# One engine instead of two for the weight splits of the expert stage of a two-layer backbone

## The chip, the cores and the metric

The kernel runs on one core of a Trainium2 chip. The metric is the device time of one execution in microseconds (us). The engines named below are TensorE (PE, matmuls), VectorE (DVE), ScalarE (ACT), GpSimd (POOL) and SyncE (SP), which only issues transfers here. SBUF is the on-chip memory that they share, PSUM the eight banks that TensorE writes.

## The reference

Two layers over 256 latent and 256 context tokens of width 1024, all in float32. Layer 0 is a gated mixer and a dense SwiGLU of width 2816. Layer 1 is an attention mixer and then a top-2-of-8 mixture of SwiGLU experts over the 256 latent tokens, each expert with three 1024 x 2816 matrices:

```python
def swiglu(h, w_gate, w_up, w_down):
    return (jax.nn.silu(h @ w_gate) * (h @ w_up)) @ w_down

def moe_swiglu(h, router, w_gate, w_up, w_down):
    ...
    for e in range(N_EXPERTS):
        y = y + gates[:, e:e + 1] * swiglu(hf, w_gate[e], w_up[e], w_down[e])
    return y.reshape(b, l, d)
```

## The kernel before

**Weights come in slabs.** Every weight matrix is cut into slabs of 128 partitions x 2048 float32 (1 MB); there are 401 of them in one order, number n. SyncE loads slab n into one of six `raw` buffers. ScalarE copies it, rounded to the matmul's format, into one of three `hi` buffers (L420, `split_hi`). Then `lo = raw - hi` is written into one of three `lo` buffers (L428, `split_lo`): VectorE does the first five eighths (128x1280), GpSimd the rest (128x768), each counting on its own semaphore, `lo_dve` and `lo_pool`. TensorE waits for both counts (`slab`, L431) and makes three matmuls of each product (`product`: hi x hi, L479, then the two cross terms, L480 and L481), so that a slab is 12 matmuls of 512 columns, or 24 of 256. The last matmul of a slab raises `slab_used`.

**What a step waits for.** ScalarE's copy of slab n waits until the slab has landed and until slab n-3 is used. Both subtractions wait for that copy. The load of slab n waits until both parts of the subtraction of slab n-6 are counted (of slab n-3 in the overflow stage, where only three `raw` buffers are in turn).

**The expert stage.** The experts go in four rounds of a loop, two per round (w = 0 and 1), 33 slabs each: six blocks c of gate and up columns (slabs 0 to 21; gate and up of block c are slabs 4c to 4c+3, the last block is slabs 20 and 21), then 11 slabs of the down matrix. Each expert has 128 token slots; the overflow stage ("over") repeats one expert for the tokens that found no slot, here once. After up block c TensorE transposes the activations of block c-1 (L1843). Between slab 21 and slab 22 it transposes block 4, gathers the tokens of the next expert with small matmuls (L1815), and transposes block 5. After slab 3 of w = 1 it scatters the result of w = 0 back to the tokens (L1866, L1867), and at the end of a round that of w = 1.

**What VectorE does beside the subtraction.** Its queue is in order. Per expert: six products with silu (`act_e`, L1394), six lo parts of the transposed activations (`act_lo`, L1404), two masks of the next gather (`place`, L1381), two lo parts of the gathered tokens (L1386), two of the output (L1411), four weighted additions (L1419). The place of each in the queue is written out:

```python
for s in range(33):
    splits(st, (w, s), it=it)
    ...
    if s in (6, 10, 14, 18, 22):
        act_e(st, w, (s - 6) // 4, it)
    if s in (10, 14, 18, 22):
        act_lo(st, w, (s - 10) // 4, it)
    if s == 12 and st == "moe":
        place(0, 1 - w, it * 2 + (w + 1))
    if s == 23:
        act_e(st, w, 5, it)
        act_lo(st, w, 4, it)
```

GpSimd does nothing in the expert and overflow stages but its part of the subtraction. The gather's second half needs the PSUM bank that `act_lo` of block 4 empties.

Of the kernel before, what the change touches and what calls it, by code (L numbers as in the profile page):

```python
# [50 lines left out]
NE = 8  # L51
# [3 lines left out]
OVER = 2 * SEQ // (SLOTS + 1)  # L55
# [8 lines left out]
RAW, SPL = 6, 3  # L64
# [154 lines left out]
def build(nc, a, out):  # L219
# [3 lines left out]
    slabs, n, landed = {}, 0, [0] * RAW  # L223
# [9 lines left out]
    banks, at, signals = {}, [0] * 8, [0] * 8  # L233
    for stage, times, uses in bank_order():
# [8 lines left out]
        at = [at[b] + times * per[b] for b in range(8)]  # L243
        signals = [signals[b] + times * per_signal[b] for b in range(8)]

    with ExitStack() as ctx:
        def sem(name):
            return ctx.enter_context(nc.semaphore(name))

        def sb(name, shape, dt=F32, into=None):  # L250
            return (into or ctx).enter_context(nc.sbuf_tensor(name, shape, dt))
# [97 lines left out]
        over = sb("over", [P, 3, NE], into=zone4)  # L349
        over_i = sb("over_i", [P, 2, NE], I32, zone4)  # L350
# [19 lines left out]
        lo_pool = [sem(f"lo_pool{i}") for i in range(SPL)]  # L370
# [19 lines left out]
        h2_hi, routed = sem("h2_hi"), sem("routed")  # L390
# [6 lines left out]
        def view(t, shape):  # L397
            k, f = shape
            return t[:, 0:k * f].rearrange("p (k f) -> p k f", k=k)

        def load(sp, stage, key, src, it=0):

            n0, per, slot, _, _, depth = slabs[stage, key]
            if n0 >= depth:
                before = (n0 - depth) // SPL + 1 + it * (per // SPL)
                sp.wait_ge(lo_dve[n0 % SPL], before)
                sp.wait_ge(lo_pool[n0 % SPL], before)
                if not isinstance(it, int):

                    sp.wait_ge(hi_ready, n0 - depth + 1)  # L410
            _, k, f = src.shape
            sp.dma_start(view(raw[slot], (k, f)), src).then_inc(raw_in[slot], 16)  # L412
# [9 lines left out]
        def split_lo(eng, stage, key, size=SLAB, it=0):  # L422

            n0, per, slot, _, _, _ = slabs[stage, key]
            at = size * 5 // 8
            cols, ready = (slice(at, size), lo_pool) if eng is nc.gpsimd else (slice(0, at), lo_dve)
            eng.wait_ge(hi_ready, n0 + 1 + it * per)
            eng.tensor_tensor(lo[n0 % SPL][:, cols], raw[slot][:, cols], hi[n0 % SPL][:, cols].bitcast(F32),  # L428
                              ALU.subtract).then_inc(ready[n0 % SPL], 1)

        def slab(pe, stage, key, shape, it=0):  # L431

            n0, per = slabs[stage, key][:2]
            there = n0 // SPL + 1 + it * (per // SPL)
            pe.wait_ge(lo_dve[n0 % SPL], there)
            pe.wait_ge(lo_pool[n0 % SPL], there)
            return view(hi[n0 % SPL], shape), view(lo[n0 % SPL], shape)

        def bank(pe, stage, key, it=0):
# [10 lines left out]
        def full(eng, stage, key, it=0):  # L450

            b, _, _, r, per, closing = banks[stage, key]
            if closing is None:
                eng.wait_ge(bank_full[b], r + 1 + it * per)
            elif stage == "ffn":
                eng.wait_ge(slab_used, ffn_slab(closing, it) + 1)
            else:
                n0, per = slabs[stage, closing][:2]
                eng.wait_ge(slab_used, n0 + 1 + it * per)
            return ps[b]  # L460
# [47 lines left out]
        def ada_stage(layer, cb):  # L508

            return "late" if layer == 1 and cb in LATE else f"ada{layer}"  # L510

        def mod_rows(st, cb):

            if st == "late":
                return late_row[0:5, :]
            return (zp if st == "ada0" and cb in (2, 3) else mrow)[0:5, cb % 2, :]

        def spread(cb, who=0):

            return ("bc", cb, who) if cb in GATE_BLOCKS else ("col", cb)  # L520

        def before(layer, cb):

            if layer == 0:
                last = {4: 0, 5: 1}.get(cb, cb - 2)
                return ("ada0", spread(last, 1)) if cb >= 4 else None
            return ("ada1", spread(cb - 2)) if cb >= 2 else ("ada0", spread(10 + cb, 1))
# [41 lines left out]
        def _(sp):  # L569
            def ada(layer, key):  # L570
                cb, h = key
                load(sp, ada_stage(layer, cb), key, columns(a["ada_w"][layer], slice(4 * h, 4 * h + 4), 512 * cb, 512 * cb + 512))
# [11 lines left out]
            for stage, key in FIRST_SLABS + MIX_SLABS:  # L584
                if stage == "ab_in":
                    load(sp, stage, key, columns(a["ab_w_in"][0], slice(0, 8), 256 * key, 256 * key + 256))
                elif stage == "ab_out":
                    h, q = key
                    load(sp, stage, key, columns(a["ab_w_out"][0], slice(4 * q, 4 * q + 4), 512 * h, 512 * h + 512))
                else:  # L590
                    ada(int(stage == "ada1"), key)
# [52 lines left out]
        @block.gpsimd  # L644
        def _(pool):
            def bias(layer, cb):

                if cb == LATE[0] and layer == 1:
                    full(pool, "ukv", (3, 1))
                elif ada_stage(layer, cb) == "late":  # L650
                    full(pool, "late", spread(cb - 1))
                elif before(layer, cb):
                    full(pool, *before(layer, cb))
                pool.dma_start(mod_rows(ada_stage(layer, cb), cb)[4:5], a["ada_b"][layer:layer + 1, 512 * cb:512 * cb + 512]
                               ).then_inc(bias_in[cb % 2], 16)

            for stage, key in FIRST_SLABS + MIX_SLABS:
                split_lo(nc.gpsimd, stage, key)
                if stage in ("ada0", "ada1") and key[1] == 1 and (stage, key) not in FIRST_SLABS:
                    bias(int(stage == "ada1"), key[0])  # L660
            for key in ("g0", "u0", "g1"):
                split_lo(nc.gpsimd, "ffn_in", key)
            with pool.Fori(0, 4) as it:
                for key in ("uA", "dA", "gA", "uB", "dB", "gB"):
                    split_lo(nc.gpsimd, "ffn_loop", key, it=it)
            for key in ("u9", "d8", "g10", "u10", "d9", "d10"):
                split_lo(nc.gpsimd, "ffn_out", key)
            for j in range(6):
                split_lo(nc.gpsimd, "cd_in", j, 8 * min(256, CDIN - 256 * j))
            for h in range(2):  # L670
                split_lo(nc.gpsimd, "uq", h, 3 * 384)
            split_lo(nc.gpsimd, "ukv", 0)
            for cb in LATE:
                for h in range(2):
                    split_lo(nc.gpsimd, "late", (cb, h))
                bias(1, cb)
            for h in range(2):
                for q in range(2):
                    split_lo(nc.gpsimd, "cd_out", (h, q))

            with pool.Fori(0, NE // 2) as it:
                for w in range(2):
                    for s in range(33):
                        split_lo(nc.gpsimd, "moe", (w, s), it=it)
            pool.wait_ge(routed, 1)
            with pool.Fori(0, OVER) as j:
                more = pool.value_load(over_i[0:1, 0, bass.ds(j, 1)], min_val=0, max_val=NE)
                with pool.If(more > 0):
                    for s in range(33):
                        split_lo(nc.gpsimd, "over", (0, s), it=j)  # L690


        @block.scalar
# [790 lines left out]
        def _(pe):  # L1484
# [24 lines left out]
            def rows_of(layer, cb, h):  # L1509

                st = ada_stage(layer, cb)
                b = bank(pe, st, ("m", cb)) if h == 0 else ps[banks[st, ("m", cb)][0]]
                wh, wl = slab(pe, st, (cb, h), (4, 512))
                for k in range(4):
                    T.matmul(b[0:4, :], C4[:, 4 * h + k, :], wh[:, k, :], start=(h == 0 and k == 0), stop=False)  # L1515
                    ins = T.matmul(b[0:4, :], C4[:, 4 * h + k, :], wl[:, k, :], start=False, stop=(h == 1 and k == 3))  # L1516
                used(ins)
# [404 lines left out]
```

## Time and profile before

| | |
|---|---|
| device time, median of 3 runs | 2097.69 us (2094.6 to 2099.28) |
| span of the profiled execution | 2090.8 us |
| what lies around the span, to the median | 6.9 us |
| TensorE matmul busy | 1869.7 us, 89% |
| VectorE busy | 1321.0 us, 63% |
| GpSimd busy | 1122.4 us, 54% |
| ScalarE busy | 990.8 us, 47% |
| expert stage | 991.3 to 1931.5 us of the span |
| overflow stage | until about 2070 us |

The profile is one execution; its own time is the span and what lies around it, which the profile does not show, so 6.9 us is the difference to the median of the other runs. A row of the trace's timeline gives the start, the duration, the engine, the line, the operation with the tiles that it writes and reads, and in brackets how long the engine had been idle and what ended that. A busy TensorE is not one at its peak, since matmuls overlap: the distance from one start to the next is what counts.

### The profile page before, as it was taken

How to read it: one execution, taken by the hardware profiler on the slowest of the kernel's cores; microseconds unless marked ns; L12 is line 12 of the kernel's file. 1: busy time of each engine (PE TensorE's matmuls, PEld its weight loads, DVE VectorE, ACT ScalarE, POOL GpSimd, SP SyncE). 2: the span in 40 equal slices, each digit the busy share in tenths (PEclk: the TensorE clock that was granted, in tenths of full speed). 3: DMA queues.
4: the chain of work that ended last, by engine and by line, in shares of the span. 5: the costliest groups of instructions: out<-in, count | busy, mean ns of one | idle time of the engine just before them, and what ended most of it. 6: DMA issues, size and time to landing. Idle time of an engine off the chain costs nothing.

```text
span 2090.8 us, 24509 instructions
## 1 busy us (share of the span) xinstructions
PE 1869.7 (89%) x8695; PEld 1435.9 (69%) x8696; DVE 1321.0 (63%) x1247; ACT 990.8 (47%) x867; POOL 1122.4 (54%) x426
## 2 busy tenths in 40 slices
PE   5888969999998778996999989999999989999785
PEld 2675648888887774665677767776777767777664
DVE  5546464243345667752877869686877869686454
ACT  5443342212211434433656556565656656564453
POOL 5345331122220212330969678786969678785684
PEclk9999989999999789996999999999999999999798
DMA  9445332232322223430879789797879889795583
GB/s 354 166 137 201 121 102 82 99 110 70 120 63 71 92 73 121 162 108 30 300 269 330 279 282 342 270 325 260 301 266 330 278 279 343 269 329 200 185 297 141
DMA packets 215161, 426.41 MB, mean 204 GB/s; under 512 B 8806, under 2 KB 64648, under 8 KB 215052
## 3 DMA queue, kind: packets, MB, share of 16 engines
q1 hardware_dynamic: 210178, 420.33, 59.1%
q10 hardware_dynamic: 4234, 4.57, 0.7%
q8 instruction: 70, 1.15, 0.2%
q14 instruction: 39, 0.32, 0.0%
q0 software_dynamic: 640, 0.04, 0.0%
HBM read 423.86 MB, written 1.05 MB: 203 GB/s over the span
## 4 chain that ended last, share of the span: by engine, by line
POOL 35%; PE 33%; issue 22%; DVE 6%; ACT 3%; DMA 1%; SPq 0%; POOLq 0%; DVEq 0%; ACTq 0%
POOL lo L428 35%; PE bank L479 9%; PE bank L480 9%; PE bank L481 9%; DVE lo L428 2%; ACT hi L420 2%; PE bank L1743 1%; PE bank L1758 1%; PE bank L1515 1%; PE bank L1516 1%; DMA raw<-in_ada_w_dram 1%; PE bank L1764 1%; PE bank L1506 1%; PE bank L1501 1%; SPq L412 0%
## 5 line engine op out<-in xcount | busy, mean ns | idle before, releaser
L428 POOL TENSOR_TENSOR lo<-raw,hi 128x768 fp32r<-128x768 f32 x401 | 1112.1, 2792 | 887.2 <-ACT hi L420 887.0
L428 DVE TENSOR_TENSOR lo<-raw,hi 128x1280 fp32r<-128x1280 f32 x401 | 864.9, 2174 | 371.1 <-ACT hi L420 370.4
L420 ACT ACTIVATE hi<-raw 128x2048 fp32r<-128x2048 f32 x401 | 763.2, 1910 | 568.4 <-PE bank L481 509.9
L479 PE MATMUL bank<-hi,xgh 128*128 128x512 f32 (+1 forms) x864 | 343.7, 398 | 34.0 <-POOL lo L428 21.9
L480 PE MATMUL bank<-lo,xgh 128*128 128x512 f32 (+1 forms) x864 | 329.1, 381 | 0.0
L481 PE MATMUL bank<-hi,xgl 128*128 128x512 f32 (+1 forms) x864 | 328.6, 380 | 0.0
L479 PEld LDWEIGHTS bank<-hi,xgh 128*128 128x128 f32 x864 | 165.4, 191 | 109.3 <-issue 58.2
L481 PEld LDWEIGHTS bank<-hi,xgl 128*128 128x128 f32 x864 | 165.5, 191 | 34.0
L480 PEld LDWEIGHTS bank<-lo,xgh 128*128 128x128 f32 x864 | 165.8, 192 | 26.4
L479 PE MATMUL bank<-hi,aTh 128*128 128x512 f32 x396 | 166.9, 421 | 4.7 <-POOL lo L428 3.1
L480 PE MATMUL bank<-lo,aTh 128*128 128x512 f32 x396 | 160.1, 404 | 0.0
L481 PE MATMUL bank<-hi,aTl 128*128 128x512 f32 x396 | 159.5, 403 | 0.0
L479 PE MATMUL bank<-Hhi,hi 128*128 128x512 f32 x352 | 139.4, 396 | 2.9 <-DVE Hlo L974 2.9
L480 PE MATMUL bank<-Hlo,hi 128*128 128x512 f32 x352 | 139.6, 397 | 0.0
L481 PE MATMUL bank<-Hhi,lo 128*128 128x512 f32 x352 | 138.9, 395 | 0.0
L1138 DVE TENSOR_TENSOR am<-bank,mrow 128x512 f32<-128x512 f32 x22 | 15.2, 692 | 189.3 <-PE bank L481 189.3
L479 PEld LDWEIGHTS bank<-hi,aTh 128*128 128x128 f32 x396 | 77.2, 195 | 47.5 <-issue 32.7
L1515 PE MATMUL bank<-hi,C 128*4 128x512 f32 x192 | 82.2, 428 | 23.7 <-POOL lo L428 13.5
L479 PE MATMUL bank<-hi,Hhi 128*128 128x256 f32 (+1 forms) x256 | 82.5, 322 | 8.3 <-issue 4.6
L481 PEld LDWEIGHTS bank<-hi,aTl 128*128 128x128 f32 x396 | 77.1, 195 | 18.6
L480 PEld LDWEIGHTS bank<-lo,aTh 128*128 128x128 f32 x396 | 77.5, 196 | 14.7
L480 PE MATMUL bank<-lo,Hhi 128*128 128x256 f32 (+1 forms) x256 | 81.5, 318 | 0.0
(308 smaller groups left out, 2484.4 us busy)
## 6 DMA issues: line engine op xcount, KB each, us to landing
raw<-in_moe_w_gate_dram SPq DMA_DIRECT2D x99, 1024.0 KB, 5.2
raw<-in_moe_w_up_dram SPq DMA_DIRECT2D x99, 1024.0 KB, 5.2
raw<-in_moe_w_down_dram SPq DMA_DIRECT2D x99, 1024.0 KB, 5.0
raw<-in_ada_w_dram SPq DMA_DIRECT2D x48, 1024.0 KB, 5.2
raw<-in_ffn_w_gate_dram SPq DMA_DIRECT2D x11, 1024.0 KB, 5.4
raw<-in_ffn_w_up_dram SPq DMA_DIRECT2D x11, 1024.0 KB, 5.4
raw<-in_ffn_w_down_dram SPq DMA_DIRECT2D x11, 1024.0 KB, 4.9
raw<-in_ab_w_in_dram SPq DMA_DIRECT2D x6, 1024.0 KB, 5.3
```

The source lines that it names most:

```text
L420: nc.scalar.activation(hi[n0 % SPL][:, 0:size], raw[slot][:, 0:size], ACT.Copy).then_inc(hi_ready, 1)
L428: eng.tensor_tensor(lo[n0 % SPL][:, cols], raw[slot][:, cols], hi[n0 % SPL][:, cols].bitcast(F32), ALU.subtract).then_inc(ready[n0 % SPL], 1)
L479: nc.tensor.matmul(dst, lh, rh, start=first, stop=False, skip_group_check=True)
L480: nc.tensor.matmul(dst, lh, rl, start=False, stop=False, skip_group_check=True)
L481: return nc.tensor.matmul(dst, ll, rh, start=False, stop=last, skip_group_check=True)
L1501: filled(T.matmul(bank(pe, st, ("bc", cb, who))[:], sel[:, who, :], row, start=True, stop=True), st, ("bc", cb, who))
L1506: ins = T.matmul(b[:, 2 * j:2 * j + 2], row[:, j * P:(j + 1) * P], sel[:, :, 0], start=True, stop=True)
L1515: T.matmul(b[0:4, :], C4[:, 4 * h + k, :], wh[:, k, :], start=(h == 0 and k == 0), stop=False)
L1516: ins = T.matmul(b[0:4, :], C4[:, 4 * h + k, :], wl[:, k, :], start=False, stop=(h == 1 and k == 3))
L1743: filled(T.matmul(bank(pe, "att", ("s", i))[:], q_, k_, start=True, stop=True), "att", ("s", i))
L1758: ins = T.matmul(b[:, 0:64], pT[:, i % 2, t * P:(t + 1) * P], val, start=(t == 0), stop=(t == 3))
L1764: ins = T.transpose(b[:, t * P:(t + 1) * P], pexp[:, (i - 1) % 2, t * P:(t + 1) * P], ident[:])
```

## The change

VectorE subtracts the whole slab (128x2048) in the stages "moe" and "over"; GpSimd's loops over these stages are gone. TensorE no longer waits for `lo_pool` there. A load in these stages waits for a constant count of `lo_pool`, that of all the slabs that are still divided; for the first three loads of the experts this is a later slab than before (the last three of the attention's output matrix in place of those three slabs earlier). All other stages keep the division.

```diff
+        ALONE = ("moe", "over")
+
+        def shared_rounds(b):
+
+            return (slabs["moe", (0, 0)][0] - 1 - b) // SPL + 1
+
         def load(sp, stage, key, src, it=0):
...
                 sp.wait_ge(lo_dve[n0 % SPL], before)
-                sp.wait_ge(lo_pool[n0 % SPL], before)
+                sp.wait_ge(lo_pool[n0 % SPL], shared_rounds(n0 % SPL) if stage in ALONE else before)
...
         def split_lo(eng, stage, key, size=SLAB, it=0):
...
-            at = size * 5 // 8
+            at = size if stage in ALONE else size * 5 // 8
...
             pe.wait_ge(lo_dve[n0 % SPL], there)
-            pe.wait_ge(lo_pool[n0 % SPL], there)
+            if stage not in ALONE:
+                pe.wait_ge(lo_pool[n0 % SPL], there)
...
-            with pool.Fori(0, NE // 2) as it:
-                for w in range(2):
-                    for s in range(33):
-                        split_lo(nc.gpsimd, "moe", (w, s), it=it)
-            pool.wait_ge(routed, 1)
-            with pool.Fori(0, OVER) as j:
-                more = pool.value_load(over_i[0:1, 0, bass.ds(j, 1)], min_val=0, max_val=NE)
-                with pool.If(more > 0):
-                    for s in range(33):
-                        split_lo(nc.gpsimd, "over", (0, s), it=j)
```

## Rows read from the trace of the kernel before

**Rows 1.** The page: the span, and the chain that ended last, by line.

```profile
span 2090.8 us, 24509 instructions
...
POOL lo L428 35%; PE bank L479 9%; PE bank L480 9%; PE bank L481 9%; DVE lo L428 2%; ACT hi L420 2%; PE bank L1743 1%; PE bank L1758 1%; PE bank L1515 1%; PE bank L1516 1%; DMA raw<-in_ada_w_dram 1%; PE bank L1764 1%; PE bank L1506 1%; PE bank L1501 1%; SPq L412 0%
```

**Rows 2.** Windows: the last round of the expert loop, and the overflow stage.

```profile
core 0: us, PE busy (x) PEld busy (x) DVE busy (x) ACT busy (x) POOL busy (x), PEclk, DMA share, GB/s
...
1696.20:1931.50 235.30, 222.00 (x969) 170.14 (x968) 183.55 (x110) 143.74 (x101) 185.30 (x66) 0.95 0.83 285
1931.50:2070.00 138.50, 114.10 (x484) 87.32 (x483) 68.32 (x56) 71.15 (x50) 102.47 (x33) 0.91 0.68 228
```

**Rows 3.** Groups of instructions in the round from 1696.2 to 1931.5 us.

```profile
L428 POOL TENSOR_TENSOR lo<-raw,hi 128x768 fp32r<-128x768 f32 x66 | 185.3, 2830 | 50.3 <-ACT hi L420 50.3
L428 DVE TENSOR_TENSOR lo<-raw,hi 128x1280 fp32r<-128x1280 f32 x66 | 153.2, 2340 | 40.6 <-ACT hi L420 40.5
```

**Rows 4.** Timeline of VectorE in expert 5 (w = 1 of the third round).

```profile
1601.33 1.49 DVE L428 TENSOR_TENSOR lo<-raw,hi 128x1280 fp32r<-128x1280 f32 x1 [1.44 <-ACT hi L420]
...
1609.72 2.29 DVE L428 TENSOR_TENSOR lo<-raw,hi 128x1280 fp32r<-128x1280 f32 x1 [0.78 <-ACT hi L420]
...
1618.08 3.68 DVE L1381 TENSOR_SCALAR Pm<-slot_row,posn 128x128 fp32r<-128x128 f32 x2
...
1654.02 0.68 DVE L1404 TENSOR_TENSOR aTl<-bank,aTh 128x512 fp32r<-128x512 f32 x1
```

**Rows 5.** Timeline of GpSimd in experts 4 and 5.

```profile
1553.22 44.72 POOL L428 TENSOR_TENSOR lo<-raw,hi 128x768 fp32r<-128x768 f32 x15 [11.71 <-ACT hi L420]
...
1650.60 1.82 POOL L428 TENSOR_TENSOR lo<-raw,hi 128x768 fp32r<-128x768 f32 x1 [1.29 <-ACT hi L420]
```

**Rows 6.** Instructions of line 1473, VectorE: min/median/max ns.

```profile
L1473 DVE TENSOR_TENSOR X<-X x2: 1219/1222/1226, 2079.9 to 2081.0; 128x1024 f32<-128x1024 f32 x2
```

**Rows 7.** Timeline of ScalarE, experts 4 and 5: copies that wait for a used slab.

```profile
1551.22 1.92 ACT L420 ACTIVATE hi<-raw 128x2048 fp32r<-128x2048 f32 x1 [4.08 <-PE bank L481]
...
1593.26 1.91 ACT L420 ACTIVATE hi<-raw 128x2048 fp32r<-128x2048 f32 x1 [1.14 <-PE bank L481]
...
1664.47 1.92 ACT L420 ACTIVATE hi<-raw 128x2048 fp32r<-128x2048 f32 x1 [3.48 <-PE bank L481]
```

**Rows 8.** Timeline of TensorE in expert 5.

```profile
1596.39 0.39 PE L479 MATMUL bank<-hi,xgh 128*128 128x512 f32 x1
...
1607.58 0.60 PE L1843 MATMUL bank<-ident,ame 128*128 128x128 f32 x4
1607.93 0.48 PE L479 MATMUL bank<-hi,xgh 128*128 128x512 f32 x1
...
1644.46 0.60 PE L1843 MATMUL bank<-ident,ame 128*128 128x128 f32 x4
...
1651.39 0.65 PE L1843 MATMUL bank<-ident,ame 128*128 128x128 f32 x4 [0.69 <-DVE ame L1394]
...
1654.75 1.11 PE L1815 MATMUL bank<-Pm,h2h 128*128 128x128 f32 x8 [1.73 <-DVE aTl L1404]
...
1693.85 0.40 PE L481 MATMUL bank<-hi,aTl 128*128 128x512 f32 x1
```

**Rows 9.** Timeline of SyncE's transfers, overflow stage; 1951.14 and 1984.02 are nine loads apart.

```profile
1951.14 0.37 SPq L412 DMA_DIRECT2D raw<-in_moe_w_up_dram  x1
...
1984.02 3.46 SPq L412 DMA_DIRECT2D raw<-in_moe_w_gate_dram  x2
```

**Rows 10.** Timeline of GpSimd: its first expert slabs.

```profile
993.31 9.22 POOL L428 TENSOR_TENSOR lo<-raw,hi 128x768 fp32r<-128x768 f32 x3 [55.32 <-ACT hi L420]
```

**Rows 11.** Windows: a burst of loads, the end of slabs 20 and 21, the gather.

```profile
1216.00:1220.00 4.00, 3.98 (x18) 2.94 (x17) 2.29 (x1) 0.33 (x1) 4.00 (x2) 1.00 1.05 388
...
1648.00:1652.00 4.00, 3.31 (x29) 3.01 (x27) 4.00 (x4) 2.53 (x3) 2.71 (x2) 1.00 0.99 358
...
1656.00:1660.00 4.00, 3.66 (x18) 3.26 (x18) 3.02 (x3) 0.88 (x2) 0.38 (x1) 0.50 0.81 266
```

## The prediction

> **What bounds the kernel now.** I read the chain that ended last first: GpSimd's part of the subtraction has 35% of the span, more than any other line [rows 1]. GpSimd is only 54% busy, so this is a limit of one stage, and the windows say which: a round of two experts takes 235.3 us, with GpSimd busy for 185.3 of them; four rounds and the overflow stage (138.5 us) are half the span [rows 2].
>
> In that stage the durations are to be read, not the shares. VectorE's 128x1280 subtraction takes 1.49 us when it starts first and 2.29 us a few slabs later, 2.34 us in the mean of 66 [rows 3, 4]. GpSimd's 128x768 takes 1.82 us alone, but 15 of them in a row with no idle time take 44.72 us, 2.98 us each [rows 5]. Each engine is slow just when the other works: one waits until the other's instruction ends. So the two parts of a slab are done one after the other, in about 3.0 us, and the division buys no overlap. The two mask instructions, on only 128 elements each, show the same: 3.68 us for both [rows 4].
>
> TensorE alone is faster than that. Where its slabs are prepared ahead, four of them take 11.19 us (1596.39 to 1607.58), 2.80 each, and the transposes behind them 0.35 us, 11.54 in all; the next three such blocks took 36.88 us (1607.58 to 1644.46), 12.29 each [rows 8]. In the down part ScalarE's copies, each of which waits for a used slab, tell the same: 14 slabs from 1551.22 to 1593.26 us, 3.00 us each [rows 7]. So TensorE is held back by 0.2 us per slab, by the pair VectorE and GpSimd.
>
> **What the change does to a slab.** GpSimd's 1.82 us of work and all mutual waiting go; VectorE gets 768 more elements. No 128x2048 subtraction is in the trace. From below: 128x1024, alone, takes 1.22 us and 128x1280 takes 1.49 us [rows 4, 6], 1.05 ns per element, so 2048 elements take 2.29 us. From above: the stage's mean of 2.34 us scaled by 1.6 is 3.74 us [rows 3]. I take 2.29 us, because the mean holds waiting for GpSimd, which then has no work.
>
> Latency first: TensorE reaches slab n 5.60 us after it has used slab n-3. The copy takes 1.92 us [rows 7], the subtraction 2.29, the handovers about 0.1: 4.3 us, 1.3 us to spare. Where a product and a transposed lo part stand between two subtractions (two instructions of at most 0.68 us, started 0.60 us apart), the next is 0.7 us late, still inside. Throughput: four slabs cost VectorE 4 x 2.29 + 1.2 = 10.4 us against TensorE's 11.54. So TensorE becomes the bound, at 2.80 us per slab.
>
> **What it is worth, per round of two experts.**
> - Three blocks of each expert: 36.88 - 3 x 11.54 = 2.26 us [rows 8], twice: 4.5 us.
> - From slab 22 of w = 0 to slab 3 of w = 1: 42.04 - 14 x 2.80 = 2.8 us [rows 7].
> - Slabs 1 to 7 of w = 0, held back in the same way by 0.2 us: 1.4 us.
> - Slabs 23 to 32 of w = 1: from the copy at 1664.47 to the last matmul, which starts at 1693.85 and occupies TensorE for 0.23 us more, 29.6 us; less 28.0 gives 1.6 us [rows 7, 8].
> - Between slabs 21 and 22 TensorE waits 0.69 us for VectorE's product and then 1.73 us for the lo part that ends at 1654.70 [rows 4, 8]. VectorE comes to these with two subtractions before it, each after GpSimd's. With its queue no longer late the first wait goes. The lo part moves only by 0.8 us: the subtraction of slab 23 in front of it waits for its copy. 0.8 us, twice: 1.6 us.
> - At the start of a round the other way: VectorE comes to slab 0 late, from its additions, when GpSimd has done its part, and its 2.29 us are 0.5 us more than what it does now. A loss of 0.5 us.
>
> Sum 11.4 us, four rounds: 46 us. The wait of TensorE at the scatter of w = 1 stays: it hangs on additions that follow the subtraction of slab 5, whose end was VectorE's own 2.29 us after its copy, as it will be.
>
> **The overflow stage.** With three buffers a load waits for the subtraction three slabs back, so load, copy and subtraction form a ring. Nine loads took 32.88 us, 10.96 us per turn of three [rows 9]. GpSimd ends 3.1 us after the copy (a third of 9.2 [rows 10]), VectorE alone will after 2.29: 0.8 us per turn, 11 turns: 9 us. At then 10.1 us per turn TensorE's 8.4 us and the transfers have room.
>
> **What moves.** The first three expert loads wait for later slabs, the last of which GpSimd finishes at 993.31 - 55.32 = 937.99 us; they are needed at about 991 us [rows 10]. At 2.7 us per load [rows 11] six take 16 us, 37 us before that: nothing. The cover would be gone if they were more than 50 us late. GpSimd issues no transfers in these stages, so nothing is queued behind its removed instructions; TensorE loses a wait, and nobody gains one.
>
> **Transfers.** At 2.80 us a slab needs 375 GB/s. In a burst, with all engines at work, they moved 388 GB/s, 2.70 us per slab; in another window, with the transfer engines 0.99 busy, only 358 GB/s, 2.93 us per slab [rows 11]. I take the first, since in the second the loads were asked for no faster, and TensorE's pauses let them refill six buffers. The Trainium skill ("SBUF — State Buffer", summary of rules) would have 358 GB/s assumed between HBM and SBUF: by it the transfers would bound, as in the rival below. The first window is above that figure.
>
> Sum: 46 + 9 = 55 us, plus 1 us in the first round and the first overflow slab, which wait for GpSimd's end and not for VectorE's: 56 us. The profiled execution goes from 2090.8 to 2035 us; with the 6.9 us around it, 2041.7 us against the median of 2097.69.
>
> **Rivals.**
> - *VectorE stays late in the gate and up part* (its extra instructions and waits for ScalarE sit between subtractions with little to spare), the down part gains. Against it: 1.1 us spare in each block. Lost: 4 x (4.5 + 1.4) = 24 us, so 2066 us.
> - *The transfers bound.* If they sustain only the 358 GB/s of that window and the lead of six buffers doesn't cover it, 264 slabs lose 0.13 us: 34 us, so 2076 us. Against it: at 0.13 us per slab, 15 slabs use up 2 us of lead, and the lead is over 10 us (a load is issued when slab n-6 is subtracted).
> - *VectorE becomes the bound, slower.* Were the subtraction really 3.74 us, the 66 of a round would take 247 us; with about 30 us of other work VectorE would need 277 us of a round of 235.3: 4 x 42 + 11 x 0.6, so 2272 us. It decides from about 2.8 us per subtraction, where four and the 1.2 us beside them fill the 12.29 us of a block. For it speaks only the mean row; against it the 1.49 us when undisturbed.
> - *No change*: 3.0 us per slab is also near what a transfer takes, and if that set the pace nothing would move. Against it: the copies wait for TensorE (the releaser in brackets), not for data [rows 7].
> - *TensorE's clock.* Between slabs 21 and 22 the granted clock falls to 0.50 (1.2 GHz instead of 2.4) after TensorE's waits [rows 11]; over a round it is 0.95 [rows 2], some 12 us lost. Shorter waits may keep it up. If a third of it goes: 16 us more, so 2026 us. It can also fall for longer. The Trainium skill ("TensorE: Matmul & The Clock Gate", what's actually happening) says that idleness lowers the clock and activity restores it; by that rule shorter waits can only help, and the same 2026 us or less would come out.
>
> **The numbers.** Forecast 0.77, late in the gate part 0.09, transfers 0.03, clock 0.06, VectorE bound 0.03, no change 0.02. The likeliest case gives 2042 us, by its own terms 2034 to 2052. The range, 2026 to 2064 us, leaves out the slow cases and most of the second one. A measurement of this kernel tells about 0.2% (4 us) from no change: faster 0.95, same 0.02, slower 0.03.
>
> **What would show it.** Right: 128x2048 subtractions of 2.29 us with no spread; copies 2.80 us apart; blocks of 11.54 us; rounds of about 224 us; both masks together well under 1 us; TensorE's wait for the product gone; an overflow turn near 10.1 us. Wrong: copies that wait for data (transfers bound), TensorE waiting for `lo` in mid-block (VectorE late), or a subtraction above 2.5 us. What I trust least is the clock between the slabs 21 and 22 and the pace of transfers over fifteen slabs at 2.80 us.

## The result, and the profile after

The changed kernel takes 2044.54 us (median of 4 runs, 2042.05 to 2049.01), the kernel before 2097.02 us beside it (4 runs, 2094.6 to 2099.28): a ratio of 0.975, 95% interval 0.9732 to 0.9768. The forecast was 2042 us (2026 to 2064).

The profiled executions lie closer together than the medians: 2047.2 us against 2090.8 [rows 1], 43.6 us. One reason is in the single times. A span and its run differ by 1.8 us, not by the 6.9 us that I had taken from comparing a span with a median; so the profiled execution of before took about 2092.6 us, less than any of its four times, and that of after 2049.01 us, the slowest of its four. Another is the part of the kernel that the change leaves alone: the first expert copy starts at 993.68 us in this profile and at 991.32 us in that of before, and in the twelve traces whose kernels subtract as before up to there it lies anywhere from 990.8 to 998.4 us. The two profiles therefore locate gains and losses to within a few us and no better.

The page of the changed kernel: span, busy times, chain by line, and two groups.

```profile
span 2047.2 us, 23725 instructions
...
PE 1840.4 (90%) x8695; PEld 1458.3 (71%) x8696; DVE 1306.3 (64%) x1247; ACT 990.3 (48%) x867; POOL 277.8 (14%) x128
...
PE bank L486 22%; PE bank L487 22%; PE bank L488 22%; DVE lo L434 4%; ACT hi L426 3%; PE bank L1811 3%; PE bank L1754 1%; PE bank L1739 1%; PE bank L1511 1%; PE bank L1512 1%; PE bank L1839 1%; DMA raw<-in_moe_w_down_dram 1%; POOL lo L434 1%; DMA raw<-in_moe_w_up_dram 1%; PE bank L1760 1%
...
L434 DVE TENSOR_TENSOR lo<-raw,hi 128x2048 fp32r<-128x2048 f32 (+1 forms) x401 | 875.2, 2191 | 340.5 <-ACT hi L426 339.1
...
L434 POOL TENSOR_TENSOR lo<-raw,hi 128x768 fp32r<-128x768 f32 (+2 forms) x104 | 267.6, 2582 | 607.1 <-ACT hi L426 606.9
```

GpSimd's subtraction had 35% of the chain [rows 1] and has 1%; the three matmuls of a product had 27% and have 66%. TensorE sets the pace, as forecast. (All line numbers are 6 or 7 higher near the subtraction and the product, 4 lower further down: 428 became 434, 479 became 486, 1404 became 1400.)

Windows of the changed kernel: the third round of the expert loop, and the overflow stage.

```profile
core 0: us, PE busy (x) PEld busy (x) DVE busy (x) ACT busy (x) POOL busy (x), PEclk, DMA share, GB/s
1442.40:1667.70 225.30, 213.91 (x970) 174.63 (x969) 175.00 (x110) 145.04 (x104) 0.00 (x0) 0.94 0.86 309
...
1893.00:2025.00 132.00, 113.21 (x483) 89.25 (x482) 86.95 (x55) 70.56 (x49) 0.00 (x0) 0.90 0.70 239
```

A round went from 235.3 us [rows 2] to 225.3, and the fourth gained as much (10.3 us from its first copy to that of the next stage); the forecast was 224. VectorE's busy time fell, from 183.6 to 175.0 us, although it took over all of GpSimd's work: what went was waiting that the records had counted as work.

Timeline of VectorE in the changed kernel, expert 5 (w = 1 of the third round, as in [rows 4]).

```profile
1592.74 0.48 DVE L1377 TENSOR_SCALAR Pm<-slot_row,posn 128x128 fp32r<-128x128 f32 x2
...
1607.77 2.29 DVE L434 TENSOR_TENSOR lo<-raw,hi 128x2048 fp32r<-128x2048 f32 x1 [0.50 <-ACT hi L426]
1609.98 0.68 DVE L1390 TENSOR_TENSOR ame<-bank,sge 128x512 f32<-128x512 f32 x1
1610.58 0.68 DVE L1400 TENSOR_TENSOR aTl<-bank,aTh 128x512 fp32r<-128x512 f32 x1
1611.18 2.28 DVE L434 TENSOR_TENSOR lo<-raw,hi 128x2048 fp32r<-128x2048 f32 x1
1613.81 2.29 DVE L434 TENSOR_TENSOR lo<-raw,hi 128x2048 fp32r<-128x2048 f32 x1 [0.35 <-ACT hi L426]
...
1623.34 2.29 DVE L434 TENSOR_TENSOR lo<-raw,hi 128x2048 fp32r<-128x2048 f32 x1 [0.43 <-ACT hi L426]
...
1625.88 0.68 DVE L1400 TENSOR_TENSOR aTl<-bank,aTh 128x512 fp32r<-128x512 f32 x1
```

Every subtraction takes 2.28 or 2.29 us, with no spread. It waits for its copy, so VectorE keeps up: after the two short instructions it is late for one slab only. The two masks take 0.48 us instead of 3.68 [rows 4].

Timeline of TensorE in the same expert: the transposes at the start and at the end of three blocks, and the gather in the transition from slab 21 to slab 22.

```profile
1582.34 0.60 PE L1839 MATMUL bank<-ident,ame 128*128 128x128 f32 x4
...
1617.26 0.60 PE L1839 MATMUL bank<-ident,ame 128*128 128x128 f32 x4
...
1623.50 1.09 PE L1811 MATMUL bank<-Pm,h2h 128*128 128x128 f32 x8
1626.62 1.39 PE L1811 MATMUL bank<-Pm,h2h 128*128 128x128 f32 x8 [2.03 <-DVE aTl L1400]
1627.81 3.62 PE L1811 MATMUL bank<-Pm,h2l 128*128 128x128 f32 x16
```

Three blocks take 34.92 us (1582.34 to 1617.26), 11.64 each, against 36.88 [rows 8]. The wait for the product at 1651.39 [rows 8] is gone. The wait for the lo part in mid-gather is not shorter but longer, 2.03 us against 1.73. The windows of this transition show what follows from it (columns as above).

```profile
1624.00:1628.00 4.00, 1.97 (x15) 1.83 (x15) 4.00 (x4) 2.67 (x3) 0.00 (x0) 0.91 0.75 269
1628.00:1632.00 4.00, 3.87 (x19) 3.47 (x18) 1.99 (x3) 0.69 (x2) 0.00 (x0) 0.50 0.92 343
1632.00:1636.00 4.00, 3.79 (x10) 3.12 (x11) 0.58 (x2) 0.68 (x2) 0.00 (x0) 0.50 0.34 137
1636.00:1640.00 4.00, 4.00 (x15) 3.14 (x15) 0.16 (x1) 1.92 (x1) 0.00 (x0) 0.81 0.00 0
```

The granted clock falls to 0.50 (1.2 GHz) and stays there into the last window, longer than before: by the trace's record of the clock this stretch lasts 10.2 us, and lasted 6.8 us before. The two copies around the transition (slabs 24 and 25) are 13.6 us apart (ScalarE, 1624.28 and 1637.88), and were 11.9 us apart. The copy of slab 24 itself had come 1.1 us sooner after that of slab 23 (2.9 us instead of 4.0), so that from slab 23 to slab 25 the transition takes 16.5 us and took 15.9.

Timeline of SyncE's transfers in the overflow stage; 1911.40, 1940.82 and 1970.69 are nine loads apart each, the first two as in [rows 9]. Then TensorE and its window later in that stage.

```profile
1911.40 0.37 SPq L418 DMA_DIRECT2D raw<-in_moe_w_up_dram  x1
...
1940.82 3.02 SPq L418 DMA_DIRECT2D raw<-in_moe_w_gate_dram  x2
...
1970.69 0.37 SPq L418 DMA_DIRECT2D raw<-in_moe_w_up_dram  x1
...
1988.45 0.44 PE L1839 MATMUL bank<-ident,ame 128*128 128x128 f32 x2 [3.53 <-DVE aTl L1400]
...
1989.00:1992.40 3.40, 3.40 (x9) 2.62 (x10) 1.93 (x2) 0.31 (x1) 0.00 (x0) 0.51 0.92 311
```

A turn of the ring takes 9.8 and then 10.0 us; it took 10.96 [rows 9] and then 10.7. That is a gain of 5.8 us over 18 loads. But the stage as a whole, from the first copy to the last, went from 114.6 to 110.7 us only.

### The profile page after: what moved, and what is told of

Its sections match the earlier page's. It is cut to its first block, busy times and chain, and to the rows that moved or that the text cites. A ratio compares the mean times of both kernels' runs of the same rounds, so it can differ in the third digit from the quotient of the medians.

```text
span 2047.2 us, 23725 instructions
## 1 busy us (share of the span) xinstructions
PE 1840.4 (90%) x8695; PEld 1458.3 (71%) x8696; DVE 1306.3 (64%) x1247; ACT 990.3 (48%) x867; POOL 277.8 (14%) x128
## 3 DMA queue, kind: packets, MB, share of 16 engines
HBM read 423.86 MB, written 1.05 MB: 208 GB/s over the span
## 4 chain that ended last, share of the span: by engine, by line
PE 79%; DVE 9%; ACT 5%; issue 3%; DMA 3%; POOL 1%; DVEq 0%; SPq 0%; ACTq 0%
PE bank L486 22%; PE bank L487 22%; PE bank L488 22%; DVE lo L434 4%; ACT hi L426 3%; PE bank L1811 3%; PE bank L1754 1%; PE bank L1739 1%; PE bank L1511 1%; PE bank L1512 1%; PE bank L1839 1%; DMA raw<-in_moe_w_down_dram 1%; POOL lo L434 1%; DMA raw<-in_moe_w_up_dram 1%; PE bank L1760 1%
## 5 line engine op out<-in xcount | busy, mean ns | idle before, releaser
L434 DVE TENSOR_TENSOR lo<-raw,hi 128x2048 fp32r<-128x2048 f32 (+1 forms) x401 | 875.2, 2191 | 340.5 <-ACT hi L426 339.1
L486 PE MATMUL bank<-hi,xgh 128*128 128x512 f32 (+1 forms) x864 | 334.3, 387 | 23.6 <-DVE lo L434 23.3
L434 POOL TENSOR_TENSOR lo<-raw,hi 128x768 fp32r<-128x768 f32 (+2 forms) x104 | 267.6, 2582 | 607.1 <-ACT hi L426 606.9
L487 PE MATMUL bank<-lo,aTh 128*128 128x512 f32 x396 | 164.3, 415 | 0.0
L487 PEld LDWEIGHTS bank<-lo,aTh 128*128 128x128 f32 x396 | 79.4, 201 | 18.3
```

The costliest lines, as they stand in the source:

```text
L486: nc.tensor.matmul(dst, lh, rh, start=first, stop=False, skip_group_check=True)
L487: nc.tensor.matmul(dst, lh, rl, start=False, stop=False, skip_group_check=True)
```

## The experiments

Ratios are to the kernel before, run on the same chip. The first tells what the overflow stage is worth; the next four what makes the divided subtraction slow; then come the margin that VectorE has, the other stages, and what is left at the transition.

**Overflow stage alone.** VectorE alone there; the expert loop divided as before, with GpSimd's loop over it back in place.

```diff
-        ALONE = ("moe", "over")
+        ALONE = ("over",)
...
```

> Only the overflow stage is subtracted by VectorE alone; the four rounds of the expert stage stay divided. Theory (the ring of load, copy and subtraction is shorter by what VectorE's 2.29 us save against GpSimd's end at 3.1 us after the copy): 4 to 9 us faster than before, 2088 to 2093 us, and the other 45 us or so of the change missing. Rival (the overflow stage gives nothing, its transfers take the gain back): 2097 us, within 3.

Measured: 2088.34 us against 2099.35, ratio 0.995 (0.9936 to 0.9965), so 10.5 us, give or take 3. The profile has 108.5 us from the first to the last copy of the stage instead of 114.6, 6.1 us. The forecast of 9 us was of the right size; the whole change leaves less of it (3.9 us) in its own profile.

**GpSimd reads beside VectorE.** The changed kernel, and for each expert slab GpSimd subtracts 128x768 elements of an unrelated tile; nobody waits for its result.

```diff
+            for i in range(33 * NE):
+                pool.wait_ge(hi_ready, first + i + 1)
...
+                nc.gpsimd.tensor_tensor(mrow[:].rearrange("p a b -> p (a b)")[:, 0:768], fgain[:, 0:768],
+                                        fgain[:, 256:1024], ALU.subtract).then_inc(beside, 1)
```

> The changed kernel, and beside it GpSimd makes one 128x768 subtraction per slab of the expert stage on data that nobody else uses, at the pace of ScalarE's copies; nobody waits for it. Theory (a VectorE and a GpSimd instruction that both read SBUF exclude each other): per slab 2.29 us of VectorE and then about 1.6 us of GpSimd, 3.9 us in place of 2.80, so about 1.0 us more for most of 264 slabs: 2230 to 2320 us, and VectorE's subtractions spread from 2.3 to about 4 us. Rival (only the wait for a slow GpSimd was lost before, they don't disturb each other): 2044 us, within 4, subtractions of 2.29 us.

Measured: 2290.02 us, ratio 1.0906 (1.0885 to 1.0927). Groups of instructions, 1000 to 1900 us:

```profile
L435 DVE TENSOR_TENSOR lo<-raw,hi 128x2048 fp32r<-128x2048 f32 x210 | 744.5, 3596 | 44.0 <-ACT hi L427 44.0
L695 POOL TENSOR_TENSOR mrow<-fgain 128x768 f32<-128x768 f32 x211 | 735.4, 3485 | 169.2 <-ACT hi L427 143.5 <-POOL mrow L695 1.3
```

The same 128x2048 instruction takes 3596 ns instead of 2290, 1.3 us more. Nothing depends on GpSimd here, so no semaphore can be the reason: the two engines take turns. A round takes 285 us.

**GpSimd writes beside VectorE.** The same place, but 600 memsets of 128x1024, which read nothing.

```diff
+            for i in range(600):
...
+                nc.gpsimd.memset(mrow[:].rearrange("p a b -> p (a b)"), 1.0).then_inc(beside, 1)
```

> The changed kernel, and beside it GpSimd fills a tile of 128x1024 that nobody uses 600 times, one after the other, in the expert stage. It reads nothing. Theory (what they exclude each other from is reading): VectorE's subtractions stay at 2.29 us and the time at 2044 us, within 4. Rival (any access of GpSimd to SBUF excludes VectorE): subtractions of over 3 us while it lasts, 2080 us or more.

Measured: 2043.66 us, ratio 0.9731 (0.9712 to 0.9749), as the change alone. Groups, the same stretch:

```profile
L435 DVE TENSOR_TENSOR lo<-raw,hi 128x2048 fp32r<-128x2048 f32 x262 | 598.8, 2290 | 151.2 <-ACT hi L427 150.8
L693 POOL MEMSET mrow<- 128x1024 f32 x595 | 568.6, 956 | 34.3
```

GpSimd is busy for 569 of these 900 us and VectorE's instruction keeps its 2290 ns. Of these two loads on GpSimd, only the one that reads stands in the way. The Trainium skill ("SBUF — State Buffer", the section on who interferes with whom) says this: a VectorE instruction with two SBUF inputs and a GpSimd instruction that reads SBUF exclude each other, one that only writes does not. Both runs agree, with 3596 and 2290 ns.

**Divided in halves.** The kernel before, 128x1024 on each engine.

```diff
-            at = size * 5 // 8
+            at = size // 2 if stage in ("moe", "over") else size * 5 // 8
```

> The kernel before with the slabs of the expert and overflow stages halved between the two engines (128x1024 each) in place of five eighths and three. Theory (the two parts are done one after the other): 256 elements go from the faster to the slower engine, per slab 3.06 - 0.27 + 0.53 = 3.3 us, 264 slabs by 0.26 and the overflow stage: 2155 to 2175 us. Rival (they overlap, so the longer part counts, some 2.4 us for 128x1024 on GpSimd): within TensorE's 2.80 us, 2097 us or faster.

Measured: 2160.86 us, ratio 1.0288 (1.0265 to 1.0311). Groups, 1100 to 1800 us:

```profile
L428 POOL TENSOR_TENSOR lo<-raw,hi 128x1024 fp32r<-128x1024 f32 x189 | 607.2, 3246 | 109.7 <-ACT hi L420 109.5
L428 DVE TENSOR_TENSOR lo<-raw,hi 128x1024 fp32r<-128x1024 f32 x186 | 448.2, 2419 | 130.9 <-ACT hi L420 130.7
```

If the two overlapped, a more even division would be faster. It is slower, because the sum counts, and GpSimd's element is the dearer one: 1.82 us for 768 [rows 5] is 2.4 ns each, VectorE's 1.05 to 1.2.

**Seven eighths.** The kernel before, 128x1792 on VectorE and 128x256 on GpSimd.

```diff
-            at = size * 5 // 8
+            at = size * 7 // 8 if stage in ("moe", "over") else size * 5 // 8
```

> The kernel before with seven eighths of each slab of the expert and overflow stages on VectorE (128x1792) and one eighth on GpSimd (128x256). Theory (the parts are done in turn, and their sum counts): VectorE about 2.0 us, GpSimd about 0.6, 2.6 us for a slab, under TensorE's 2.80; TensorE is the bound as in the changed kernel, 2040 to 2055 us. Rival (any division costs what the mutual waiting costs, and only GpSimd's silence brings the gain): 2070 us or more.

Measured: 2034.5 us, ratio 0.9707 (0.9683 to 0.9731), faster than expected. Timeline of VectorE, then of GpSimd:

```profile
1605.12 2.03 DVE L428 TENSOR_TENSOR lo<-raw,hi 128x1792 fp32r<-128x1792 f32 x1 [0.77 <-ACT hi L420]
...
1605.16 2.58 POOL L428 TENSOR_TENSOR lo<-raw,hi 128x256 fp32r<-128x256 f32 x1 [0.22 <-ACT hi L420]
```

GpSimd's record of 2.58 us is mostly waiting: it ends 0.6 us after VectorE, and that is the duration of its 256 elements. The slab is ready 0.3 us later than with VectorE alone, and TensorE's block is 11.64 us in both, so these 0.3 us cost nothing. Its experts with w = 0 take what the changed kernel's take, those with w = 1 (the first three) 2 to 5 us less: 112.0 to 114.6 us from first copy to first copy, against 116.7. The transition of expert 5:

```profile
1617.67 1.11 PE L1815 MATMUL bank<-Pm,h2h 128*128 128x128 f32 x8 [1.76 <-DVE aTl L1404]
```

The wait in mid-gather is 1.76 us against 2.03, and the trace's record of the clock tells where the time went. At the transitions with w = 1 the half-speed stretch lasts 6.8 us in three of the four rounds and is missing in the second, the one with 112.0 us; in the first profile of the change it lasts 10.2 us in all four. That this is not one lucky execution is seen from the mean granted clock: 0.933 to 0.937 in the four runs of this kernel, 0.924 to 0.929 in all nine of the changed kernel.

**More work for VectorE.** The changed kernel, with a 128x636 subtraction of an unrelated tile on VectorE ahead of each expert slab's own.

```diff
...
+                        V.tensor_tensor(spare[:, s % 3, :] if s % 3 < 2 else mrow[:].rearrange("p a b -> p (a b)")[:, 0:636],
+                                        fgain[:, 0:636], fgain[:, 388:1024], ALU.subtract)
```

> The changed kernel with 0.74 us more of VectorE per slab of the four rounds: a subtraction of 128x636 on data that nobody uses, before the slab's own. Theory (with the change TensorE is the bound and VectorE has 0.6 us per slab to spare; beyond that VectorE takes over): VectorE needs 2.95 us per slab and 13.0 us per block of four against TensorE's 11.64, so 15 to 17 us per round and 2095 to 2120 us, back to the time of before the change. Rival (VectorE is far from being the bound, 70% busy in the round): within 10 us of 2044.

Measured: 2126.62 us, ratio 1.0149 (1.0127 to 1.017), 7 us above the expected range. TensorE, first matmul of two slabs and the transposes that end a block:

```profile
1659.23 0.50 PE L487 MATMUL bank<-hi,xgh 128*128 128x512 f32 x1 [1.00 <-DVE lo L435]
1662.14 0.60 PE L1846 MATMUL bank<-ident,ame 128*128 128x128 f32 x4
1672.16 0.50 PE L487 MATMUL bank<-hi,xgh 128*128 128x512 f32 x1 [1.01 <-DVE lo L435]
1675.06 0.60 PE L1846 MATMUL bank<-ident,ame 128*128 128x128 f32 x4
...
1686.03 1.97 PE L1818 MATMUL bank<-Pm,h2h 128*128 128x128 f32 x8 [2.75 <-DVE aTl L1401]
```

A block now takes 12.92 us (1662.14 to 1675.06). Each VectorE instruction starts 0.08 us before the end recorded for the one ahead of it (1609.98 against 1607.77 + 2.29, above), so the added one, 0.81 us by its mean, costs 0.73 and the slab's own 2.21: 4 x 2.94 + 1.2 = 13.0 us. VectorE is the bound. This is past the point where the rival "slower" of the prediction begins. What I had left out of the range is the transition: its wait grew from 2.03 to 2.75 us, and the copies of slabs 23 and 25 are 1.1 to 1.5 us further apart than in the changed kernel, 10.2 us over the eight experts, enough for the 7 us beyond the range.

**VectorE alone in all stages.**

```diff
...
-            at = size if stage in ALONE else size * 5 // 8
-            cols, ready = (slice(at, size), lo_pool) if eng is nc.gpsimd else (slice(0, at), lo_dve)
+            cols, ready = slice(0, size), lo_dve
...
```

> VectorE subtracts the whole slab in every stage; GpSimd only issues its small transfers. Theory (the mutual exclusion costs wherever slabs come faster than one per 3.1 us, which is at the start): the first 34 slabs gain 5 to 20 us; in the attention, where VectorE works most of the time, 0.8 us more per slab may be lost again on 20 slabs: 2025 to 2050 us. Rival (outside the expert stage the subtraction hides under TensorE or the transfers): 2044 us, within 4.

Measured: 2040.46 us, ratio 0.9741 (0.9717 to 0.9764): no difference from the change that can be told. By the copies of its profile against those of the changed kernel it gains some 7 us in the first 34 slabs and 6 more up to slab 81, and loses about 11 in the attention stages, where VectorE has other work in front of its subtractions. Its expert rounds, in which the two kernels are the same, are 5.5 us shorter in that profile. That is the clock again: at its first four transitions the half-speed stretch lasts 6.8 us and at the last four 10.2, while TensorE's wait is 2.03 us at all eight.

**Order at the transition.** The changed kernel; VectorE does the last product and the lo part that TensorE waits for ahead of the subtraction of slab 23, not behind it, and in the expert loop ScalarE empties the first bank of the gather ahead of its copy of slab 24.

```diff
                 for s in range(33):
+                    if s == 24 and st == "moe":
+                        gathered(st, w, it, (0,), False)
                     split_hi(act, st, (w, s), it=it)
...
                 for s in range(33):
+                    if s == 23:
+                        act_e(st, w, 5, it)
+                        act_lo(st, w, 4, it)
                     splits(st, (w, s), it=it)
...
-                    if s == 23:
-                        act_e(st, w, 5, it)
-                        act_lo(st, w, 4, it)
```

> The changed kernel with another order between slabs 21 and 22: VectorE makes the product of block 5 and the lo part of block 4 before the subtraction of slab 23, and ScalarE frees the first bank of the gather before its copy of slab 24. Theory (TensorE's wait of 2.0 us for the lo part is VectorE's queue, which has slab 23 in front): 1.7 us per expert, 8 experts, 14 us: 2026 to 2034 us, and less if the clock falls for longer. Rival (the wait hangs on the copies, not on the order): 2044 us, within 4.

Measured: 2024.43 us, ratio 0.9669 (0.9645 to 0.9693). The time is 20 us less than that of the change, but the two were not run side by side; by the ratios it is 17 us less (12 by the later ratio of the change, 0.9724). TensorE at the same transition, and two windows of it (columns as above):

```profile
1609.83 1.09 PE L1814 MATMUL bank<-Pm,h2h 128*128 128x128 f32 x8
1611.48 1.11 PE L1814 MATMUL bank<-Pm,h2h 128*128 128x128 f32 x8 [0.57 <-DVE aTl L1403]
1612.43 1.05 PE L1814 MATMUL bank<-Pm,h2l 128*128 128x128 f32 x8
...
1612.00:1616.00 4.00, 2.59 (x22) 2.31 (x21) 4.00 (x3) 1.83 (x2) 0.00 (x0) 0.94 0.35 101
1616.00:1620.00 4.00, 3.52 (x10) 2.73 (x11) 1.45 (x3) 0.77 (x2) 0.00 (x0) 0.50 1.02 413
```

The wait falls from 2.03 to 0.57 us, and the gather's matmuls run at the full clock (1.05 us for eight, not half of 3.62). The clock still falls, but for less time: its mean over the kernel is 0.937 instead of 0.926. How much of the gain in the experts belongs to VectorE's order and how much to ScalarE's was not separated. In the overflow stage only VectorE's order is changed, and there the copies of slabs 20 and 25 are 17.4 us apart instead of 21.3.

**The same order in the other kernels.** With VectorE alone in all stages, in the kernel before, and in the seven-eighths kernel. The edits are those above, put together.

> The last two together. If they are independent the gains against 2044 us add, 2010 to 2035 us.

> The kernel before with the order of the run e7_order and the division kept. Theory (the wait of 1.73 us before the gather's second half is the order of VectorE's queue, in either kernel): 1.5 us per expert, 10 to 20 us faster than before, 2078 to 2088 us. Rival (the order helps only where VectorE works alone, since here its queue is late anyway): within 4 us of before.

> Seven eighths and one eighth, as in the run e9_seven_eighths, with the order of e7_order. Theory (both keep TensorE the bound and shorten only what stands between slabs 21 and 22; the order takes most of what the shorter subtraction gives there): 2016 to 2026 us, with or a little below e7_order's 2024 us. Rival (the gains add in full, 10 and 20 us): 2014 us or less.

Measured: 2026.25 us, ratio 0.9666 (0.9643 to 0.9689); 2084.85 us, 0.995 (0.9932 to 0.9969); 2024.46 us, 0.9637 (0.9618 to 0.9657). All three lie in what was expected. The order is worth 14 us, 10 us and, by the ratios, 15 us. The last has the lowest ratio of this study, though its interval meets those of the two kernels with the order and VectorE alone.

**The change once more,** on the chip of the seven-eighths kernel with the order. No edit.

> The changed kernel once more, on the chip of the run beside it. If what e9_seven_eighths won on it (10 us) was the chip and the day, its ratio to the kernel before is now 0.971 or less; if it is the kernel, 0.975 again, 2042 to 2048 us.

Measured: 2043.0 us (2036.6 to 2046.79), ratio 0.9724 (0.9704 to 0.9745). The time lies in the second expectation, the ratio between the two, and its interval meets that of seven eighths, so whether these beat VectorE alone by much stays open; the mean clocks above speak for it. Its profile is worth more than its time. Expert 1 (w = 1 of the first round) took 112.5 us there, from first copy to first copy, against 116.7 us in the other profile of the same kernel. The transition of that expert, here TensorE and a window of this run:

```profile
1176.64 1.11 PE L1811 MATMUL bank<-Pm,h2h 128*128 128x128 f32 x8 [1.92 <-DVE aTl L1400]
1177.59 1.96 PE L1811 MATMUL bank<-Pm,h2l 128*128 128x128 f32 x16
...
1160.00:1200.00 40.00, 37.63 (x208) 32.10 (x207) 30.55 (x21) 25.58 (x20) 0.00 (x0) 1.00 0.71 258
```

and of the first profile of the change (its 40 us begin 4 us later; the transition lies in both):

```profile
1176.21 1.53 PE L1811 MATMUL bank<-Pm,h2h 128*128 128x128 f32 x8 [2.03 <-DVE aTl L1400]
1177.55 3.62 PE L1811 MATMUL bank<-Pm,h2l 128*128 128x128 f32 x16
...
1164.00:1204.00 40.00, 37.64 (x189) 32.28 (x188) 26.77 (x18) 22.28 (x17) 0.00 (x0) 0.87 0.61 218
```

One kernel, the same instructions, the waits 0.11 us apart: once the clock stayed at 1.00 and sixteen matmuls took 1.96 us, once it fell and they took 3.62. That one stretch is worth 4.2 us, and there are eight such transitions. The length of the wait doesn't decide it: in the same trace three other transitions have a wait of 1.92 us and a half-speed stretch of 10.2 us. The scatter of a few us between runs has at least part of its cause here; another part lies ahead of the experts, as said of the result.

## Why the prediction was right, point by point

**The mechanism** was right, and is shown rather than argued: VectorE's and GpSimd's subtractions take turns (3596 ns beside an unrelated reader, 2290 beside a writer, a slower kernel with halves). The price of a 128x2048 subtraction, 2.29 us from two smaller ones, was exact.

**Blocks.** Forecast 11.54 us, measured 11.64: at the transposes the next copy comes 3.24 us after the last one, not 3.15. Six blocks of a round gained 3.9 us instead of 4.5.

**Down part.** From slab 22 to slab 3 of the next expert 14 slabs took 42.04 us and take 39.09 (copies at 1528.67 and 1567.76): 2.95 us, forecast 2.8. The end of w = 1, from the copy of slab 25 to the second of the next round: 33.54 to 31.61 us, 1.9 us, forecast 1.6.

**The start of a round,** with slabs 1 to 7 and the blocks and transition of w = 0: from the first copy to the wait at slab 22 the forecast terms add up to 1.4 - 0.5 + 2.26 + 0.8 = 4.0 us; measured 4.2.

**The transition of w = 1** is the step that failed. I had 0.8 us of gain there. The wait for the product went, but TensorE then reached the gather sooner, before the lo part was there, and the wait in mid-gather grew from 1.73 to 2.03 us. The half-speed stretch grew from 6.8 to 10.2 us in each of the four rounds. Up to the copy of slab 24 the step gained 1.1 us, behind it it lost 1.7: a loss of 0.6 us instead of a gain of 0.8. (For w = 0, where the stretch is 10.2 us before and after, the same step gained 0.7 to 1.0 in the four rounds.) I had priced the clock only as something that might come back; the sentence that it "can also fall for longer" had no number. From the rule of the Trainium skill that I weighed ("TensorE: Matmul & The Clock Gate", what's actually happening: idleness lowers the clock, activity restores it) I had concluded that shorter waits could only help. The conclusion failed here: of two waits one went and the other grew, 2.4 us of waiting became 2.0, and the clock was low for longer. That the grown wait is the cause is likely, not shown, since the same wait of 2.03 us also stands beside a stretch of 6.8 us (VectorE alone in all stages). Against the 11.4 us forecast the rounds gained 10.1 to 10.6 (41.1 us over four, not 46).

**The overflow stage.** 9 us forecast. Alone it measures 10.5 us by the ratio and 6.1 us in the profile; within the whole change the profile has 3.9 us. The ring gained 5.8 us over 18 loads. Given back was some 3 us between slabs 20 and 25, 18.3 to 21.3 us, where VectorE's longer subtraction of slab 23 stands in front of the lo part. TensorE waits 3.53 us for it there (row above; 2.09 us before), and the clock then falls to 0.51. In the second profile of the same kernel the stage takes 108.6 us, so 2 us of this term are scatter.

**The prefetch, the masks, the removed instructions** cost nothing, as forecast: the first expert copy follows the last copy of the attention stages after 58.6 us, and did after 58.5 before.

**The total.** 56 us forecast, 52.5 us by the medians, 43.6 us in the first pair of profiles. The first pair adds up as 41.1 us in the rounds, 3.9 in the overflow stage and 1.0 at the end, less 2.4 us ahead of the experts, where the change does nothing. The second profile of the change (2041.2 us) makes it 49.6: 46.6 in the rounds, 6.0 in the overflow stage, 0.9 at the end and 3.8 lost ahead of the experts. So the 56 us were some 4 us too many, and the median came out 2.5 us above the forecast. My 6.9 us are 1.8 us around the span and 5.1 us by which the profiled execution was faster than the median. The forecast was right to add both, since it is to be compared with a median: 2097.69 less 56 is the same 2041.7. Only their name was wrong.

**The rivals.** VectorE late in mid-block, transfers as the bound, VectorE as the bound: none came. Transfers kept up with 2.79 us per slab, 376 GB/s over 14 slabs. Adding 0.74 us per slab did make VectorE the bound and the kernel slower, so that rival's mechanism was real, and its turning point lies below the 2.94 us per slab of that run. Its price was of the right size too: where GpSimd's reads stretched the subtraction to 3.60 us the kernel took 2290 us, against the rival's 2272 for 3.74. What it had wrong is that nothing stretched the subtraction here. The clock rival was real in the other direction: the longer stretches took back some 7 us (four times 1.7), and the change of order that shortens the wait won 12 to 17 us by the ratios.

**Still open:** how much better one eighth on GpSimd is than none (0.9707 against 0.975 and 0.9724), and what decides whether and for how long the clock falls at a transition, since the same wait goes with stretches of different length.

## What to carry to other kernels

Where an elementwise job with two inputs is divided between VectorE and GpSimd, compare the duration of each part when it starts alone with its mean: if both are longer only when the other works, the parts add up and the faster engine should have nearly all of it. When the bound moves to TensorE, look next at the short waits that break its stream, since one of 2 us before small matmuls can cost another 4 us through the clock; moving what it waits for ahead of an unhurried instruction was worth 10 to 17 us here, up to a third of the change itself. And when two executions of one kernel differ by a few us, compare the record of the clock at the same place before looking for another cause.

## What the runs showed of the hardware

GpSimd's profiled duration contains the time for which VectorE holds it off: 128x256 elements show 2.58 us, of which 0.6 are its own (what it ends after VectorE, and a third of 1.82), and a 128x768 subtraction shows 3.49 us in the mean beside VectorE's whole slabs against 1.82 for one alone [rows 5]. Beside a GpSimd that only writes, 63% busy, VectorE's instruction has the same mean as without it, 2290 ns. And the granted clock is not the same from run to run at one place of one kernel: 1.00 and 0.87 over 40 us around the same transition.
